# Sparse attention stage of a fused two-block kernel: the attention jobs begin inside the turning of the query heads, the compressed branch is cut into pieces between jobs, and a small product moves from VectorE to GpSimd

## The chip, the cores and the metric

One core of one Trainium2 chip runs the whole program. The metric is device time in microseconds (us), median of the runs shown. Engines: TensorE (PE) with its weight loads (PEld), VectorE (DVE), ScalarE (ACT), GpSimd (POOL), and SyncE (SP), which issues the weight DMAs.

## The reference, cut to what matters

The program computes two transformer-like blocks on 256 tokens of width 1024. The change touches one mixer of the second block, a sparse attention of 16 query heads (64 wide) over 4 key/value heads with three branches and a gate for each:

```
qg = u @ w_qg
q = _rmsnorm(qg[..., :N_HEADS * HEAD_DIM].reshape(...), q_norm)
gates = jax.nn.sigmoid(qg[..., N_HEADS * HEAD_DIM:].reshape(...))
o_cmp, p_slc = _compressed_branch(q, k_cmp, v_cmp, rel_bias)   # 15 blocks of keys
o_slc = _selected_branch(q, k_slc, v_slc, idx, rel_bias)       # here all 4 blocks of 64 are selected
o_win = _window_branch(q, k_win, v_win, rel_bias)              # window 512 > 256 tokens
o = gates[..., 0:1] * o_cmp + gates[..., 1:2] * o_slc + gates[..., 2:3] * o_win
return o.reshape(bsz, seq, D_MODEL) @ w_o
```

With 256 tokens the selected and the window branch are both plain causal attention, each with its own keys and values; the compressed branch attends to 15 compressed keys.

## The kernel before, in words

The tokens are two tiles (t = 0, 1) of 128. Matmuls with weights are done in three passes of split float32 (hi and lo parts); the attention is in float32. Weights come in units of 128x1024 elements through a ring of 6: SP loads a unit once its slot's `w_hi` and `w_lo` are made, ACT makes `w_hi` (`hi_parts`, L330), DVE makes `w_lo` (`lo_parts`, L338), PE uses it (`pe_chunk`, L386 to L388).

The order of the work of each engine is written out by hand; the engines wait for one another through semaphores (`done` and `when`). PSUM has 8 banks, taken in turn from three pools: A (banks 0 to 3), S (4, 5) and T (6, 7). A bank is taken again only after its last reader.

The stage (`pe_nsa`, `act_nsa`, `dve_nsa`):

1. PE projects queries and gates (chunks `qg.0`, `qg.1`, `qg.gates`, the last one 48 columns wide). DVE normalizes the queries.
2. `pe_heads` (L868): 16 transposes in four groups `nsa.q` 0 to 3, through the T banks; ACT copies each group out to `qT` (`heads_out`, L877), labels `nsa.qT0` to `nsa.qT3`. Meanwhile DVE makes `w_lo` of five units of the next weights (L2845).
3. Compressed scores: 16 matmuls with all 128 rows, in two T banks (L2738; each float32 matmul has two records). DVE adds the bias, takes the maximum and subtracts it (L2854 to L2860), ACT takes exp (L2803), DVE sums, inverts, multiplies with the gate and scales (`compressed_scaled`, L2871 to L2877).
4. 32 jobs (`nsa_jobs`), 16 for tile 0 with 128 keys and then 16 for tile 1 with 256 keys. A job is a pair of heads in one of the two branches (br). For each: PE scores (`pe_scores`, L523, 64 rows, both heads, one S bank each), DVE bias and maximum (`dve_max`, L557, L560), ACT exp (`act_exp`, L543), DVE reciprocal and its product with the gate (`dve_scale`, L576, L581), POOL scales the probabilities (`pool_attend`, L593), PE turns them (`pe_turn`, L532), ACT copies them out (`act_turned`, L601), PE multiplies with the values (`pv`, L2750, 64 columns wide) into the output banks. Both S banks are written by each job, so scores of job j+1 wait for L557 of job j.
5. `pe_attend` interleaves: scores of job j+3, then an optional piece from `between[j]`, then the turn of job j, then values of job j-1. In `between[0]` stand the compressed probabilities' transposes (L2761), in `between[1]` the 32 matmul records of the compressed output (L2771), which also start the output banks. `dve_attend` runs `between[j]`, `dve_scale(j)`, `dve_max(j+2)`; `act_attend` runs `act_exp(j+2)`, `between[j]`, `act_turned(j)`.
6. ACT and DVE split the output banks into `x_hi` and `x_lo` (L2814, L2883), and PE multiplies with `w_o` (chunks `wo_nsa.0` and `.1`).

Of the kernel before, what the change touches and what calls it, by code (L numbers as in the profile page):

```python
# [12 lines left out]
ALU = mybir.AluOpType  # L13
# [3 lines left out]
P = 128  # L17
# [103 lines left out]
def build(nc, book, d, out, bias_rows):  # L121
    ctx = ExitStack()
    done, when = book.done, book.when
    with ctx:
# [444 lines left out]
        def dve_scale(dve, tag, j, job):  # L569

            dve.wait_ge(*when(f"{tag}.exp{j}.1"))
            if job["late"] is not None:
                nc.vector.reciprocal(job["late"], soft[:, j % len(job["slots"]), 0, 1, :]).then_inc(*done("softmax_dve", f"{tag}.r{j}"))
                return
            r = soft[:, j % len(job["slots"]), 1, 2, :]
            nc.vector.reciprocal(r, soft[:, j % len(job["slots"]), 0, 1, :]).then_inc(*done("softmax_dve", f"{tag}.r{j}"))  # L576
            dve.wait_ge(*when(f"{tag}.r{j}"))
            if job["gate"] is not None:
                r2 = soft[:, j % len(job["slots"]), 1, 1, :]

                nc.vector.tensor_tensor(r2, r, job["gate"], ALU.mult).then_inc(*done("softmax_dve", f"{tag}.g{j}"))  # L581
                return
            for i in range(2):
                p = slot(j, job, 1)[:, i, 0:job["nk"]]
                nc.vector.tensor_scalar(p, p, r[:, i:i + 1], None, ALU.mult
                                        ).then_inc(*done("softmax_dve", f"{tag}.p{j}.{i}"))

        def pool_attend(pool, tag, jobs):

            for j, job in enumerate(jobs):  # L590
                pool.wait_ge(*when(f"{tag}.g{j}"))
                p = slot(j, job, 1)[:, :, 0:job["nk"]]
                nc.gpsimd.tensor_tensor(p, p, bc(soft[:, j % len(job["slots"]), 1, 1, :], 2, job["nk"]), ALU.mult  # L593
                                        ).then_inc(*done("softmax_pool", f"{tag}.p{j}.1"))
# [9 lines left out]
        def pe_attend(pe, tag, jobs, pv, between={}):  # L604
# [4 lines left out]
            for j in range(m):  # L609
# [250 lines left out]
        def pe_heads(pe, tag, src, n, width, ready):  # L860

            for a in range(n // 2):
                for x in ready(a) if callable(ready) else ready if a == 0 else ():
# [1841 lines left out]
        def nsa_jobs():  # L2705
            assert SEQ // 64 <= 8 and SEQ <= 512
            jobs = []
            for t in range(T):
                for a in range(NH // 2):
                    for br in range(2):  # L2710
# [5 lines left out]
                            late=None, bias=BT[:, 2 * a:2 * a + 2, SEQ - nk:SEQ], slots=slots_nsa, ready=[], a=a, t=t, br=br))  # L2716
# [8 lines left out]
        def pe_nsa(pe):  # L2725
# [3 lines left out]
            pe_heads(pe, "nsa.q", lambda t, i: q_nat2[:, t, i * P:(i + 1) * P], NH // 2, P,  # L2729
                     lambda a: [f"nsa.qn{a}"])  # L2730

            pe.wait_ge(*when("nsa.qT3"))
            pe.wait_ge(*when("cmp.kT1"))
            for t in range(T):
                b = take(pe, "T", f"cmp.scores{t}")
                for a in range(NH // 2):
                    o = psum[:, b, 32 * a:32 * a + 32].rearrange("p (i c) -> p i c", i=2)
                    last = nc.tensor.matmul(o[:, :, 0:n_blocks(t)], qT[:, a, t * P:(t + 1) * P],  # L2738
                                            kcTz[:, :, NCMP * (a // 2):NCMP * (a // 2) + n_blocks(t)], start=True, stop=True)
                last.then_inc(*done("cmp_pe", f"cmp.s{t}"))  # L2740
            o_banks = [[take(pe, "A", f"nsa.o{t}{x}") for x in range(2)] for t in range(T)]
            jobs = nsa_jobs()

            def pv(pe, j):
# [3 lines left out]
                for i in range(2):  # L2748
                    for kb in range(nb):
# [3 lines left out]
                            start=False, stop=True, skip_group_check=True)  # L2753
                return last

            def compressed_turn():
                for t in range(T):
                    pe.wait_ge(*when(f"cmp.p{t}"))
                    b = take(pe, "T", f"cmp.ptb{t}")
                    for x in range(2):  # L2760
                        last = nc.tensor.transpose(psum[:, b, x * P:(x + 1) * P],  # L2761
                                                   xc[:, t, 8 * x:8 * x + 8, :].rearrange("p h c -> p (h c)"), ident[:])
                    last.then_inc(*done("cmp_pe", f"cmp.pt{t}"))

            def compressed_out():
                pe.wait_ge(*when("cmp.pT1"))
                pe.wait_ge(*when("cmp.vc1"))

                for t in range(T):
                    for a in range(NH // 2):  # L2770
                        nc.tensor.matmul(psum[:, o_banks[t][a // 4], (a % 4) * P:(a % 4 + 1) * P],  # L2771
                                         vcz[:, 2 * a:2 * a + 2, :].rearrange("p i d -> p (i d)"), pcT[:, t, a // 4, :],
                                         start=(a % 4 == 0), stop=True, skip_group_check=True)

            pe_attend(pe, "nsa.sm", jobs, pv, between={0: compressed_turn, 1: compressed_out})
# [4 lines left out]
        def act_nsa(act):  # L2780
# [19 lines left out]
            for t in range(T):  # L2800
# [3 lines left out]
            def compressed_turned():  # L2804
                for t in range(T):
                    act.wait_ge(*when(f"cmp.pt{t}"))
                    nc.scalar.activation(pcT[:, t], bank(f"cmp.ptb{t}")[:, 0:2 * P].rearrange("p (a k) -> p a k", a=2), ACT.Copy
                                         ).then_inc(*done("cmp_act", f"cmp.pT{t}", frees=(f"cmp.ptb{t}",)))

            act_attend(act, "nsa.sm", nsa_jobs(), between={0: compressed_turned})  # L2810
# [10 lines left out]
        def dve_nsa(dve):  # L2821
# [23 lines left out]
            lo_parts(dve, chunk_end("qg.gates") + RING - 1)  # L2845
            dve.wait_ge(loads["bias_in"], 16 * P // SHIFTED)
            dve.wait_ge(*when("nsa.xc0"))
            dve.wait_ge(*when("nsa.late"))
            for t in range(T):
# [11 lines left out]
            def compressed_scaled():  # L2861
                for t in range(T):
                    x = xc[:, t, :, 0:n_blocks(t)]
                    m, r = cm[:, 2 * t], cm[:, 2 * t + 1]
    
                    def step(ins, label):
                        ins.then_inc(*done("cmp_dve", label))
                        dve.wait_ge(*when(label))
    
                    dve.wait_ge(*when(f"cmp.e{t}"))  # L2870
                    step(nc.vector.tensor_reduce(m, x, AX.X, ALU.add), f"cmp.sum{t}")  # L2871
                    step(nc.vector.reciprocal(r, m), f"cmp.r{t}")
                    dve.wait_ge(*when("nsa.gate1"))
                    step(nc.vector.tensor_tensor(m, r, gate[:, t, :, 0], ALU.mult), f"cmp.g{t}")
                    if t == 0:
                        step(nc.vector.tensor_scalar(m, m, late, None, ALU.mult), "cmp.late")
                    step(nc.vector.tensor_tensor(x, x, bc(m, 2, n_blocks(t)), ALU.mult), f"cmp.p{t}")  # L2877

            dve_attend(dve, "nsa.sm", nsa_jobs(), between={0: compressed_scaled})
# [152 lines left out]
```

## Time and profile before

| what | value |
|---|---|
| median of 3 runs | 1487.38 us (1486.51 to 1488.74) |
| profiled execution | 1487.94 us, its span 1486.2 us |
| PE busy | 1409.9 us, 95% of the span |
| DVE, ACT, POOL busy | 851.4, 807.4, 325.4 us |
| mean granted TensorE clock | 0.963 |

The span is the time from the first to the last instruction of the profiled execution; the time around it is 1.7 us. The stage that is changed lies between 1190 and 1272 us of the span. A TensorE clock of 1.00 is 2.4 GHz, of 0.50 is 1.2 GHz.

### The profile page before, as it was taken

How to read it: one execution, taken by the hardware profiler on the slowest of the kernel's cores; microseconds unless marked ns; L12 is line 12 of the kernel's file. 1: busy time of each engine (PE TensorE's matmuls, PEld its weight loads, DVE VectorE, ACT ScalarE, POOL GpSimd, SP SyncE). 2: the span in 40 equal slices, each digit the busy share in tenths (PEclk: the TensorE clock that was granted, in tenths of full speed). 3: DMA queues.
4: the chain of work that ended last, by engine and by line, in shares of the span. 5: the costliest groups of instructions: out<-in, count | busy, mean ns of one | idle time of the engine just before them, and what ended most of it. 6: DMA issues, size and time to landing. Idle time of an engine off the chain costs nothing.

```text
span 1486.2 us, 21916 instructions
## 1 busy us (share of the span) xinstructions
PE 1409.9 (95%) x7306; PEld 1164.9 (78%) x7306; DVE 851.4 (57%) x1240; ACT 807.4 (54%) x1322; POOL 325.4 (22%) x368
## 2 busy tenths in 40 slices
PE   8998989999879999959899999999999989999998
PEld 6887878887758887848778888888888875788887
DVE  5537665446566655657665555555555569455554
ACT  7776566674665555322664444765444548464442
POOL 2011000011159979927310000010000005000000
PEclk9998999999989999966899999999999969999999
DMA  9532535522455654210685565478656420356661
GB/s 333 170 95 72 212 114 179 154 92 76 138 142 188 190 164 136 99 29 15 207 263 185 185 191 188 153 158 219 192 185 193 137 72 2 114 184 186 195 185 56
DMA packets 170926, 224.73 MB, mean 151 GB/s; under 512 B 15881, under 2 KB 113393, under 8 KB 170849
## 3 DMA queue, kind: packets, MB, share of 16 engines
q1 hardware_dynamic: 168016, 217.27, 46.0%
q0 software_dynamic: 2160, 6.02, 2.6%
q8 instruction: 47, 0.77, 0.2%
q10 hardware_dynamic: 672, 0.42, 0.1%
q14 instruction: 31, 0.25, 0.1%
HBM read 221.16 MB, written 1.44 MB: 150 GB/s over the span
## 4 chain that ended last, share of the span: by engine, by line
PE 84%; DVE 7%; ACT 4%; POOL 3%; issue 2%; DMA 0%; SPq 0%; ACTq 0%; DVEq 0%; POOLq 0%
PE psum L1609 14%; PE psum L1597 11%; PE psum L1599 11%; PE psum L1598 11%; PE psum L386 8%; PE psum L388 8%; PE psum L387 8%; PE psum L523 2%; PE psum L412 2%; DVE w_lo L338 1%; PE psum L1636 1%; POOL w_raw L2017 1%; PE psum L532 1%; PE psum L2750 1%; PE psum L2550 1%
## 5 line engine op out<-in xcount | busy, mean ns | idle before, releaser
L1796 DVE TENSOR_TENSOR w_lo<-w_raw,w_hi 128x1024 fp32r<-128x1024 f32 x216 | 283.8, 1315 | 288.1 <-ACT w_hi L1730 287.8
L1730 ACT ACTIVATE w_hi<-w_raw 128x1024 fp32r<-128x1024 f32 x216 | 228.8, 1060 | 309.3 <-PE psum L1599 217.4
L338 DVE TENSOR_TENSOR w_lo<-w_raw,w_hi 128x1024 fp32r<-128x1024 f32 (+4 forms) x191 | 225.6, 1208 | 121.5 <-ACT w_hi L330 120.2
L1597 PE MATMUL psum<-w_hi,x_hi 128*128 128x512 f32 x704 | 280.8, 399 | 1.5 <-DVE x_lo L438 0.7
L1599 PE MATMUL psum<-w_hi,x_lo 128*128 128x512 f32 x704 | 275.3, 391 | 0.0
L1598 PE MATMUL psum<-w_lo,x_hi 128*128 128x512 f32 x704 | 274.8, 390 | 0.0
L330 ACT ACTIVATE w_hi<-w_raw 128x1024 fp32r<-128x1024 f32 (+4 forms) x191 | 193.2, 1038 | 109.8 <-PE psum L388 63.1
L386 PE MATMUL psum<-w_hi,x_hi 128*128 128x512 f32 (+5 forms) x608 | 232.9, 383 | 3.3 <-DVE x_lo L2883 2.3
L388 PE MATMUL psum<-w_hi,x_lo 128*128 128x512 f32 (+5 forms) x608 | 228.3, 375 | 0.0
L387 PE MATMUL psum<-w_lo,x_hi 128*128 128x512 f32 (+5 forms) x608 | 227.9, 375 | 0.0
L1599 PEld LDWEIGHTS psum<-w_hi,x_lo 128*128 128x128 f32 x704 | 132.5, 188 | 28.6
L1597 PEld LDWEIGHTS psum<-w_hi,x_hi 128*128 128x128 f32 x704 | 132.6, 188 | 28.2 <-issue 1.3
L1598 PEld LDWEIGHTS psum<-w_lo,x_hi 128*128 128x128 f32 x704 | 132.8, 189 | 26.0
L386 PEld LDWEIGHTS psum<-w_hi,x_hi 128*128 128x128 f32 x608 | 115.7, 190 | 24.0 <-DVE x_lo L2883 2.6
L388 PEld LDWEIGHTS psum<-w_hi,x_lo 128*128 128x128 f32 x608 | 115.7, 190 | 20.3
L387 PEld LDWEIGHTS psum<-w_lo,x_hi 128*128 128x128 f32 x608 | 115.9, 191 | 18.3
L1609 PE MATMUL psum<-w_hi,f_hi 128*128 128x512 f32 x320 | 100.6, 396 | 3.1 <-DVE f_lo L1790 3.1
L1609 PE MATMUL psum<-w_lo,f_hi 128*128 128x512 f32 x320 | 99.1, 391 | 0.0
L1609 PE MATMUL psum<-w_hi,f_lo 128*128 128x512 f32 x320 | 99.1, 391 | 0.0
L593 POOL TENSOR_TENSOR arena<-arena,soft 128x256 f32<-128x256 f32 (+1 forms) x32 | 26.5, 827 | 246.7 <-DVE soft L581 246.7
L438 DVE SCALAR_TENSOR_TENSOR x_lo<-psum,gain,x_hi 128x256 fp32r<-128x256 f32 x104 | 44.4, 476 | 47.4 <-ACT x_hi L422 47.4
L1609 PEld LDWEIGHTS psum<-w_hi,f_hi 128*128 128x128 f32 x320 | 59.5, 190 | 15.3 <-DVE f_lo L1790 3.5
(404 smaller groups left out, 1823.3 us busy)
## 6 DMA issues: line engine op xcount, KB each, us to landing
w_raw<-in_ffn_w_in SPq DMA_DIRECT2D x352, 256.0 KB, 3.2
w_raw<-in_ffn_w_out SPq DMA_DIRECT2D x176, 256.0 KB, 2.8
w_raw<-in_w_in SPq DMA_DIRECT2D x88, 256.0 KB, 3.5
w_raw<-in_w_out SPq DMA_DIRECT2D x32, 256.0 KB, 3.7
w_raw<-in_w_kv SPq DMA_DIRECT2D x24, 256.0 KB, 2.9
w_raw<-in_mem_wk SPq DMA_DIRECT2D x16, 256.0 KB, 5.7
w_raw<-in_mem_wv SPq DMA_DIRECT2D x16, 256.0 KB, 4.8
w_raw<-in_mem_wq SPq DMA_DIRECT2D x16, 256.0 KB, 6.3
```

Of the source, the lines that this page charges most:

```text
L330: nc.scalar.activation(w_hi[:, s, 0:size(u)], w_raw[:, s, 0:size(u)], ACT.Copy).then_inc(hi_ready, 1)
L338: nc.vector.tensor_tensor(w_lo[:, s, 0:size(u)], w_raw[:, s, 0:size(u)], w_hi[:, s, 0:size(u)].bitcast(F32), ALU.subtract).then_inc(lo_rea ...
L386: nc.tensor.matmul(o, xh, whi, start=(k + i == x_first), stop=False)
L387: nc.tensor.matmul(o, xh, wlo, start=False, stop=False)
L388: last = nc.tensor.matmul(o, xl, whi, start=False, stop=(k + i == x_first + kts - 1))
L438: ins = nc.vector.scalar_tensor_tensor(lo, pb, g[:, k:k + 1], hi, ALU.mult, ALU.subtract)
L1597: nc.tensor.matmul(o, xh, whi, start=(kt == 0), stop=False)
L1598: nc.tensor.matmul(o, xh, wlo, start=False, stop=False)
L1599: last = nc.tensor.matmul(o, xl, whi, start=False, stop=(kt == KT - 1))
L1609: last = nc.tensor.matmul(psum[:, FF_ACC[2 * t + n], :], x, w[:, n * 512:(n + 1) * 512], start=(first and w is whi and x is xh), stop=Fals ...
L1730: nc.scalar.activation(w_hi[:, s, :], w_raw[:, s, :], ACT.Copy).then_inc(hi_ready, 1)
L1796: nc.vector.tensor_tensor(w_lo[:, s, :], w_raw[:, s, :], w_hi[:, s, :].bitcast(F32), ALU.subtract).then_inc(lo_ready, 1)
```

## The change

- `pe_heads` gets a `between` argument. Scores of job 0 are issued before group 2 of the query transposes, scores of job 1 before group 3, and `pe_attend` begins with job 2 (`begun=2`). Jobs of tile 0 and branch 0 wait for their `nsa.qT` group.
- The compressed scores go into two A banks (which later serve as the output banks of tile 1) in four pieces at jobs 2 to 5; the transposes of the compressed probabilities at jobs 11 and 13; the compressed output in four pieces at jobs 13 to 16. The first value matmul of tile 0 in each bank now starts the bank.
- ACT and DVE do their parts of the compressed branch at the jobs shown.
- DVE makes two units of `w_lo` instead of five before the attention; the other three follow after it.
- The product of reciprocal and gate is done by POOL, just before its scaling, instead of DVE.

```diff
@@ dve_scale
             nc.vector.reciprocal(r, soft[..., 0, 1, :]).then_inc(*done("softmax_dve", f"{tag}.r{j}"))
+            if job["gate"] is not None:
+                return
             dve.wait_ge(*when(f"{tag}.r{j}"))
-            if job["gate"] is not None:
-                r2 = soft[:, j % len(job["slots"]), 1, 1, :]
-                nc.vector.tensor_tensor(r2, r, job["gate"], ALU.mult).then_inc(*done("softmax_dve", f"{tag}.g{j}"))
-                return
@@ pool_attend
+                pool.wait_ge(*when(f"{tag}.r{j}"))
+                nc.gpsimd.tensor_tensor(g, r, job["gate"], ALU.mult).then_inc(*done("softmax_pool", f"{tag}.g{j}"))
                 pool.wait_ge(*when(f"{tag}.g{j}"))
@@ pe_attend
-            for j in range(m):
+            for j in range(begun, m):
                 pe_scores(pe, tag, j, jobs[j])
@@ nsa_jobs
-                            ... ready=[], a=a, t=t, br=br))
+                            ... ready=[f"nsa.qT{a // 2}"] if t == br == 0 else [], a=a, t=t, br=br))
@@ pe_nsa
-            pe_heads(pe, "nsa.q", ..., lambda a: [f"nsa.qn{a}"])
-            (all compressed scores here, in two T banks)
+            pe_heads(pe, "nsa.q", ..., lambda a: [f"nsa.qn{a}"],
+                     between={2: lambda: pe_scores(pe, "nsa.sm", 0, jobs[0]), 3: lambda: pe_scores(pe, "nsa.sm", 1, jobs[1])})
+            score_bank = [take(pe, "A", f"cmp.scores{t}") for t in range(T)]
+            o_banks = [[take(pe, "A", f"nsa.o0{x}") for x in range(2)], score_bank]
...
-                            start=False, stop=True, skip_group_check=True)
+                            start=(t == 0 and a % 4 == 0 and job["br"] == 0 and kb == 0), stop=True, skip_group_check=True)
...
-            pe_attend(pe, "nsa.sm", jobs, pv, between={0: compressed_turn, 1: compressed_out})
+            compressed = {2: lambda: compressed_scores(0, 0), 3: lambda: compressed_scores(0, 1),
+                          4: lambda: compressed_scores(1, 0), 5: lambda: compressed_scores(1, 1),
+                          11: lambda: compressed_turn(0), 13: lambda: [compressed_turn(1), compressed_out(0, 0)],
+                          14: lambda: compressed_out(0, 1), 15: lambda: compressed_out(1, 0), 16: lambda: compressed_out(1, 1)}
+            pe_attend(pe, "nsa.sm", jobs, pv, between=compressed, begun=2)
@@ act_nsa
-            act_attend(act, "nsa.sm", nsa_jobs(), between={0: compressed_turned})
+            act_attend(act, "nsa.sm", nsa_jobs(), between={6: lambda: compressed_exp(0), 8: lambda: compressed_exp(1),
+                                                           12: lambda: compressed_turned(0), 14: lambda: compressed_turned(1)})
@@ dve_nsa
-            lo_parts(dve, chunk_end("qg.gates") + RING - 1)
+            lo_parts(dve, chunk_end("qg.gates") + 2)
...
-            dve_attend(dve, "nsa.sm", nsa_jobs(), between={0: compressed_scaled})
+            dve.wait_ge(*when("nsa.gate1"))
+            dve_attend(dve, "nsa.sm", nsa_jobs(), between={5: lambda: compressed_max(0), 7: lambda: compressed_max(1),
+                                                           9: lambda: compressed_scaled(0), 11: lambda: compressed_scaled(1)})
```

`compressed_scores(t, half)` is 4 of the 8 compressed score matmuls of tile t, `compressed_out(t, x)` 4 of its 8 output matmuls, `compressed_turn(t)` its two transposes; the operations themselves are those of before.

## Rows read from the trace of the kernel before

**Rows 1.** The page: PE busy, and the granted clock in 40 slices.
```profile
PE 1409.9 (95%) x7306; PEld 1164.9 (78%) x7306; DVE 851.4 (57%) x1240; ACT 807.4 (54%) x1322; POOL 325.4 (22%) x368
...
PEclk9998999999989999966899999999999969999999
```

**Rows 2.** Stretches: length, busy us (instructions) of each engine, granted clock, DMA.
```profile
668.00:688.00 20.00, 19.78 (x127) 17.79 (x128) 15.08 (x22) 3.71 (x7) 15.08 (x14) 0.50 0.00 1
139.30:149.40 10.10, 10.05 (x36) 8.66 (x36) 6.96 (x17) 6.40 (x26) 4.60 (x3) 0.50 0.27 56
1193.96:1200.79 6.83, 6.81 (x33) 6.30 (x33) 6.36 (x13) 4.69 (x8) 0.00 (x0) 0.50 0.02 4
1204.20:1221.27 17.07, 12.07 (x57) 10.06 (x57) 9.55 (x33) 5.27 (x21) 2.46 (x4) 0.50 0.29 95
1221.27:1272.40 51.13, 47.72 (x411) 29.91 (x411) 40.69 (x115) 43.04 (x148) 24.00 (x28) 1.00 0.01 1
1272.47:1275.88 3.41, 3.41 (x10) 2.65 (x9) 0.47 (x1) 0.00 (x0) 0.00 (x0) 0.50 0.41 121
```

**Rows 3.** Timeline of PE: start, length, operation, idle time before.
```profile
1197.32 3.77 PE L868 MATMUL psum<-ident,arena 128*128 128x128 f32 x16
1201.86 4.93 PE L2738 MATMUL psum<-arena 128*128 128x14 f32 x32 [0.78 <-ACT arena L877]
...
1213.97 0.80 PE L523 MATMUL psum<-arena 64*128 64x128 f32 x4 [3.03 <-DVE arena L557]
...
1215.96 0.66 PE L532 MATMUL psum<-ident,arena 128*128 128x128 f32 x2
...
1217.28 5.73 PE L2771 MATMUL psum<-arena 128*128 128x128 f32 x32
1222.84 0.38 PE L532 MATMUL psum<-ident,arena 128*128 128x128 f32 x2
```

**Rows 4.** Compressed scores (L2738) at full clock: length, PE busy (records), clock.
```profile
1201.86:1204.20 2.34, 2.34 (x21) 1.00 0.93 283
```

**Rows 5.** Compressed output (L2771) at half clock, same columns.
```profile
1217.85:1221.27 3.42, 3.42 (x18) 0.50 0.00 0
```

**Rows 6.** The chain of waits, one tile-0 job, and the first turn of tile 1.
```profile
1224.01 0.37 PE psum L532 x2
1224.38 0.37 PE psum L2750 x4
1224.75 0.42 PE psum L523 x4
...
1241.77 0.59 PE psum L532 x4
```

**Rows 7.** Timeline of DVE.
```profile
1198.40 5.76 DVE L338 TENSOR_TENSOR w_lo<-w_raw,w_hi 128x1024 fp32r<-128x1024 f32 x5
...
1206.83 0.56 DVE L2854 SCALAR_TENSOR_TENSOR arena<-psum,arena 128x240 f32<-128x240 f32 x1 [1.80 <-PE psum L2738]
...
1208.18 0.42 DVE L557 SCALAR_TENSOR_TENSOR arena<-psum,arena 128x256 f32<-128x256 f32 x1
...
1211.75 0.40 DVE L2871 TENSOR_REDUCE arena<-arena 128x16 f32<-128x240 f32 x1
...
1213.13 0.17 DVE L576 RECIPROCAL soft<-soft 128x2 f32<-128x2 f32 x1
...
1226.21 0.16 DVE L581 TENSOR_TENSOR soft<-soft,arena 128x2 f32<-128x2 f32 x1
```

**Rows 8.** Timeline of ACT.
```profile
1201.83 1.28 ACT L2803 ACT_TABLE_LOAD   x1
...
1209.08 0.40 ACT L543 ACTIVATE arena<-arena,soft 128x128 f32<-128x128 f32 x1 [0.38 <-DVE soft L560]
```

**Rows 9.** POOL's groups by shape: busy us, mean ns, idle before.
```profile
L593 POOL TENSOR_TENSOR arena<-arena,soft 128x256 f32<-128x256 f32 x16 | 9.8, 614 | 235.3 <-DVE soft L581 235.3
L1935 POOL TENSOR_SCALAR arena<-arena 128x1 f32<-128x1 f32 x1 | 0.2, 187 | 0.1
```

More of the change, by code:

```diff
@@ L858, in pe_mem_kv, with pe_heads @@
             pe_heads(pe, f"memk{l}", lambda t, i: mk_nat[:, t, i * P:(i + 1) * P], MEM_H, P, [f"memk{l}.nat1"])
-        def pe_heads(pe, tag, src, n, width, ready):
+        def pe_heads(pe, tag, src, n, width, ready, between={}):
             for a in range(n // 2):
+                if a in between:
+                    between[a]()
                 for x in ready(a) if callable(ready) else ready if a == 0 else ():
@@ L2728, in pe_nsa @@
             pe_chunk(pe, "qg.gates")
[L2729 to L2741, printed above, removed]
             jobs = nsa_jobs()
+            pe_heads(pe, "nsa.q", lambda t, i: q_nat2[:, t, i * P:(i + 1) * P], NH // 2, P, lambda a: [f"nsa.qn{a}"],
+                     between={2: lambda: pe_scores(pe, "nsa.sm", 0, jobs[0]), 3: lambda: pe_scores(pe, "nsa.sm", 1, jobs[1])})
+            score_bank = [take(pe, "A", f"cmp.scores{t}") for t in range(T)]
+            o_banks = [[take(pe, "A", f"nsa.o0{x}") for x in range(2)], score_bank]
             def pv(pe, j):
@@ L2765, in compressed_out @@
[L2765 to L2773, printed above, removed]
@@ L2775, in pe_nsa, with compressed_scores @@
-            pe_attend(pe, "nsa.sm", jobs, pv, between={0: compressed_turn, 1: compressed_out})
+            def compressed_scores(t, half):
+                if t == half == 0:
+                    pe.wait_ge(*when("nsa.qT3"))
+                    pe.wait_ge(*when("cmp.kT1"))
+                for a in range(4 * half, 4 * half + 4):
+                    o = psum[:, score_bank[t], 32 * a:32 * a + 32].rearrange("p (i c) -> p i c", i=2)
+                    last = nc.tensor.matmul(o[:, :, 0:n_blocks(t)], qT[:, a, t * P:(t + 1) * P],
+                                            kcTz[:, :, NCMP * (a // 2):NCMP * (a // 2) + n_blocks(t)], start=True, stop=True)
+                if half:
+                    last.then_inc(*done("cmp_pe", f"cmp.s{t}"))
@@ new lines, in compressed_turn, with compressed_out @@
+            def compressed_turn(t):
+                pe.wait_ge(*when(f"cmp.p{t}"))
+                free_bank(pe, score_bank[t], f"cmp.ptb{t}")
+                for x in range(2):
+                    last = nc.tensor.transpose(psum[:, score_bank[t], x * P:(x + 1) * P],
+                                               xc[:, t, 8 * x:8 * x + 8, :].rearrange("p h c -> p (h c)"), ident[:])
+                last.then_inc(*done("cmp_pe", f"cmp.pt{t}"))
+            def compressed_out(t, x):
+                if x == 0:
+                    pe.wait_ge(*when(f"cmp.pT{t}"))
+                    pe.wait_ge(*when("cmp.vc1"))
+                if t:
+                    free_bank(pe, o_banks[t][x], f"nsa.o{t}{x}")
+                for a in range(4 * x, 4 * x + 4):
+                    nc.tensor.matmul(psum[:, o_banks[t][x], (a % 4) * P:(a % 4 + 1) * P],
+                                     vcz[:, 2 * a:2 * a + 2, :].rearrange("p i d -> p (i d)"), pcT[:, t, x, :],
+                                     start=(t == 1 and a % 4 == 0), stop=True, skip_group_check=True)
@@ L2799, in act_nsa, with compressed_exp @@
             heads_out(act, "act", "nsa.q", qT, NH // 2, P, "nsa.qT", scale=gcol["qk"][:, 0:1])
-            for t in range(T):
+            def compressed_exp(t):
                 act.wait_ge(*when(f"cmp.sub{t}"))
```

60 lines of the change are left out of this document (26 added, 34 removed).

## The prediction

> **What bounds the kernel now.** I read the page first: PE is busy 95% of the span, and the clock line falls to 6 in the slice that holds the changed stage [rows 1]. Then the stretches with their clock, then the timelines of the stage. From 1193.96 to 1272.40 two regimes are seen. From 1204.20 to 1221.27 TensorE has 1.2 GHz and works 12.07 of 17.07 us; from 1221.27 on it has 2.4 GHz and works 47.72 of 51.13 us [rows 2]. In the first regime little is done: the compressed scores (4.93 us), four job scores with waits up to 3.03 us for L557, and the compressed output (5.73 us) [rows 3]. In the second the chain of waits runs on PE alone: turn 0.37, values 0.37, scores 0.42, so 1.16 us for a tile-0 job [rows 6]. So until the turn of job 1 at 1222.84 latency and the low clock bound the stage, and after it PE's own work does. From the turn of job 1 to that of job 16 (1241.77) it is 18.9 us, 15 x 1.16 = 17.4 plus 1.5 where the tile changes [rows 3, 6].
>
> **The start.** Eight query transposes at 3.77/16 = 0.24 us, the scores of job 0 at 0.80, four transposes: PE is at about 1201.0. DVE, with two conversions of 5.76/5 = 1.15 us instead of five, is free at 1200.7, does L557 (0.42), and lets the scores of job 1 go at 1201.2 [rows 3, 7]. At full clock these take 0.42 [rows 6], the last four transposes (half of 0.94) 0.5, and PE has finished them and the scores of job 2 by 1202.7. ACT's last copy-out then ends about 1203.0, where it ended at 1201.8; the table load (1.28) moves with it, so the first exp is at 1204.3 instead of 1209.08 [rows 8]. Two exps (0.8), reciprocal (0.17), L557 (0.42): the scores of job 3 at 1205.8, and the turn of job 0 at 1206.6, where it was 1215.96 [rows 3, 7, 8]. The turn of job 1 follows at 1208.0, where it was 1222.84 [rows 3]. That is 14.8 us earlier. It is not the gain: all compressed pieces are still to come.
>
> **What is put back between the jobs, at full clock.** Compressed scores: 32 records at 2.34/21 = 0.11 us, 3.6 us [rows 4]. Compressed transposes: four, as two tile-0 turns, 0.7 us [rows 6]. Compressed output: 32 records, 0.19 us each at half clock [rows 5], so 0.10 to 0.11 at full, 3.5 us. DVE: both S banks are refilled by each job, so what DVE does between two L557 delays PE's next scores unless PE has something else. The first maximum piece lies beside PE's compressed scores, free. The second costs 1208.18 - 1206.83 = 1.35 us and each scaling piece 1213.13 - 1211.75 = 1.38 [rows 7]; DVE's own work for a job is about 0.9 of the 1.16, so about 1.1 us of each shows on PE, 3.3 us. Where all is hidden it is 0, where nothing is 4.1. The output pieces at jobs 13 to 16 cover the 1.5 us of the tile change. Sum: 3.6 + 0.7 + 3.5 + 3.3 - 1.5 = 9.6, so the turn of job 16 comes 14.8 - 9.6 = 5.2 us earlier. The 16 jobs of tile 1 are unchanged.
>
> **The same at half clock.** Here a tile-0 job costs scores 0.80, turn 0.66 [rows 3], and values, which no row shows at half clock: between 0.37 (the row at full clock) and twice that; I take 0.70, since the other two nearly double. That is 2.16 us. A job with a compressed score piece costs 8 x 0.21 = 1.7 more, 3.9 us (0.21 is twice rows 4). So from the turn of job 1 at 1208.0 four such steps lead to the turn of job 5 at 1223.5, and every further tile-0 job loses 1.0 us against before. The DVE pieces (about 0.9 + 1.38 = 2.3 in a job) nearly vanish beside 2.16. If the clock rises at the turn of job 6 (about 1225), the rest at full clock brings the turn of job 16 to 1243.9, 2.2 us later than before. If it rises only when the full-width output products come at jobs 13 and 14, it is at 1251, 9.5 us later. One at job 9 gives 4.3, one at jobs 10 to 11 gives 6.6.
>
> **Which of the two.** The clock before the change falls twice here: at 1193.96 after matmuls 48 columns wide that fully occupied PE, and at 1204.20 after a wait of 0.78 us and matmuls of 14 columns [rows 2, 3]. It rises twice: at 1200.79 after full-width transposes back to back, and at 1221.27 after the 128x128 output products had run back to back since 1217.28 [rows 2, 3, 5]. After the change PE has about 1.7 us of transposes and scores of 64 rows between 1200.8 and 1202.7, then it waits until 1205.8 for the first exp. I expect the clock to fall at 1204.20 as before. And what follows is narrow: scores of 64 rows, values 64 columns wide, compressed scores of 14 and 30 columns. Being busy isn't enough: from 668 to 688 PE was busy 19.78 of 20 us and stayed at 0.50, and in the attention at 139.30 to 149.40 10.05 of 10.10 us at 0.50 [rows 2]. What raised the clock before was the block of output products, and the change cuts that block up and puts it last. So the likeliest is half clock through jobs 2 to 5 and on for some jobs more, with the rise between job 6 and job 14: the end 2.2 to 9.5 us later. I take the middle, 6 us later.
>
> The Trainium skill, TensorE: Matmul & The Clock Gate, "What's actually happening", says that sustained activity releases the throttle. By it the low clock would end soon after the jobs run densely; that is a rival below. Rows 2 at 668 and 139.30 speak against it. The same page, "PE-mode transpose", says that transposes don't count as busy for the gate. The trace disagrees: the rise at 1200.79 came after transposes alone.
>
> **The smaller parts.** POOL's product on two elements isn't in the trace. Its nearest row is 0.187 us for one column; the upper bound is a whole scaling, 0.614 [rows 9]. I take 0.19. It replaces 0.16 on DVE [rows 7], so the probabilities are ready about 0.1 us later (up to 0.5), and POOL has 0.61 + 0.19 plus a short wait of 1.16, so it hides; at the end of the last job 0.1 shows. DVE's relief of 0.2 us a job gains nothing on a chain that runs on PE, at most 0.3 where DVE paces the tile change. The three conversions moved behind the attention, 3.5 us of DVE [rows 7], and the six DMAs of their ring slots, lie beside the `w_o` products: ten matmuls took 3.41 us at half clock [rows 2], so two ready units of 12 matmuls last at least 4 us even at full clock, and the third is converted 1.2 us after DVE is free. Cost 0; if the cover were gone, 3.5. The later loads are wanted six units on. The half-clock stretch at 1272.47 to 1275.88 [rows 2] may come or not with the shifted end: plus or minus 1.7. `between[0]` and `between[1]` are empty now, their waits are gone, with what stood behind them (turns of jobs 0 and 1), counted above.
>
> The Trainium skill, SBUF — State Buffer, "SBUF: two separate sides", says that a DVE instruction with two SBUF inputs and a GpSimd instruction block each other on a shared port pair. Six compressed DVE instructions of this kind now lie beside POOL's 0.61 us. As an estimate by that rule they could add up to 6 x 0.6 = 3.7 us, and the end would be 9 to 10 us later instead of 6. No row of before shows the two together.
>
> **Rivals.**
>
> - *The clock stays up.* If the startup's work at 1200.8 to 1202.7 and from 1205.8 on suffices, or the low clock ends at once, PE gets the sum at full clock: 5.2 us earlier (3.8 if it is low until the turn of job 2), about 1482.5. For it: the dense tile-0 jobs from 1224 on held 1.00 [rows 2]. Against it: the wait of 3 us, and the compressed score pieces. 17%. The skill's rule of sustained activity leads to the same times by another road; I give that road 8% more.
> - *A draw.* The clock rises just as the score pieces end, at job 3 to 6. Later jobs gain back what the start lost: between 2.2 earlier and 2.3 later, about 1487.5. 15%.
> - *The clock doesn't come back at all in the attention.* Then each tile-1 job would cost nearly double its 1.8 us, 16 x 1.6 = 26 us, about 1522. The output products at jobs 13 to 16 speak against it. 3%.
> - *The DVE to POOL hand-over becomes the bound*: 0.5 us per job where POOL's small product costs 0.6; 32 jobs x 0.1 to 0.3 exposed, 3 to 9 us on top of whichever clock. POOL's 0.187 row speaks against it. 4%, and it would end slower.
>
> **How the numbers follow.** The likeliest case (about 53%): the profiled execution's 1487.94 plus 6 is 1493.9; it stood 0.56 above the median of the runs, so 1493.4 for a median. Its own range is 1489.5 to 1498. The range with the other cases goes from 1482.5 (clock up) to 1499 (rise at job 14, or the port rule's and the POOL bound's additions); about 1 in 5 lies outside. 0.2% is 3.0 us, about what a measurement of this kernel can tell from no change. Faster by more: 25%, nearly all of it the clock rival. Within: the draw and the early edge of the likeliest case, 18%. Slower: 57%.
>
> **What would show it.** Right: the clock rows of the changed kernel have 0.50 from 1204 to beyond 1225, the turn of job 0 near 1206.6, tile-0 jobs 2.2 us apart and 3.9 with score pieces, tile-1 jobs again 1.82. Wrong: 1.00 from 1207 or 1211 on with jobs 2 to 5 about 2.05 us apart; POOL's small product above 0.3 us; PE waiting for POOL in front of L532; waits for `w_lo` after 1270.

## The result and the profile after

| | before | after |
|---|---|---|
| median of 7 runs (lowest to highest) | 1486.51 us (1483.48 to 1490.37) | 1495.26 us (1489.70 to 1497.98) |
| profiled execution, span | 1487.94 us, 1486.2 us | 1495.26 us, 1493.6 us |
| mean granted TensorE clock | 0.963 | 0.955 |
| PE busy | 1409.9 us | 1420.3 us |
| stage: first matmul 48 columns wide to first `w_o` matmul | 81.4 us | 88.8 us |

The changed kernel is slower by half a per cent: ratio 1.0048, 95% interval 1.0033 to 1.0064. 1493.4 us was forecast. In the two profiled executions the stage accounts for the whole difference of the spans: 1190.44 to 1271.85 us before, 1190.64 to 1279.46 after, 7.4 us more.

The page of the changed kernel, to be read beside [rows 1]: PE is busy for 10.4 us more with the same 7306 matmuls, so the matmuls themselves got longer. The clock line has 5 and 8 in the two slices of the stage where it had 6 and 9.

```profile
PE 1420.3 (95%) x7306; PEld 1170.7 (78%) x7306; DVE 844.7 (57%) x1208; ACT 807.3 (54%) x1322; POOL 331.9 (22%) x400
...
PEclk9998999999989999967899999999999958999999
```

The stretches of the changed kernel answer to [rows 2] (length, busy us and instructions of PE, PEld, DVE, ACT, POOL, then the granted clock). Before, two stretches at 0.50 were 6.83 and 17.07 us long. Now there is one of 47.79 us, and PE works 44.92 us of it:

```profile
1193.76:1241.55 47.79, 44.92 (x218) 31.38 (x218) 26.44 (x76) 25.64 (x90) 12.01 (x30) 0.50 0.07 23
1241.55:1279.10 37.55, 34.69 (x305) 22.77 (x303) 24.86 (x52) 29.50 (x89) 20.53 (x34) 1.00 0.01 1
1279.10:1282.50 3.40, 3.04 (x7) 2.48 (x8) 3.40 (x4) 0.00 (x0) 0.00 (x0) 0.50 0.14 34
```

The chain of waits of the changed kernel shows the steps one by one. First the beginning, then a job with a score piece, a job without one, the first output products (L2775), beside which the clock rises, and a job of tile 1:

```profile
1204.22 1.28 ACT L543
1205.50 0.01 issue
1205.52 0.89 ACT arena L543 x4
...
1207.06 0.80 PE psum L523 x4
1207.86 0.62 PE psum L532 x2
...
1213.52 0.63 PE psum L2743 x4
1214.15 0.73 PE psum L523 x4
1214.88 1.81 PE psum L2755 x8
1216.70 0.51 PE psum L532 x2
...
1232.46 0.63 PE psum L2743 x4
1233.08 0.73 PE psum L523 x4
1233.81 0.62 PE psum L532 x2
...
1241.20 1.12 PE psum L2775 x8
1242.32 0.22 PE psum L532 x2
...
1251.27 0.59 PE psum L2743 x8
1251.87 0.63 PE psum L523 x4
1252.50 0.59 PE psum L532 x4
```

The turn of job 0 is at 1207.8, 8.2 us ahead of the 1215.96 before [rows 3]. The turn of job 16 is at 1249.1, 7.4 us behind the 1241.70 before. Between the two a job without a piece takes 1.97 us (values 0.63, scores 0.73, turn 0.62), not 1.16 [rows 6], and one with a score piece 3.68. From job 16 on both kernels take 1.82 us a job.

### The profile page after: what moved, and what is told of

It is laid out like the page before. It is cut to its first block, busy times and chain, and to the rows that moved or that the text cites. A ratio compares the mean times of both kernels' runs of the same rounds, so it can differ in the third digit from the quotient of the medians.

```text
span 1493.6 us, 21915 instructions
## 1 busy us (share of the span) xinstructions
PE 1420.3 (95%) x7306; PEld 1170.7 (78%) x7306; DVE 844.7 (57%) x1208; ACT 807.3 (54%) x1322; POOL 331.9 (22%) x400
## 4 chain that ended last, share of the span: by engine, by line
PE 84%; DVE 6%; ACT 4%; POOL 3%; issue 2%; DMA 1%; SPq 0%; ACTq 0%; DVEq 0%; POOLq 0%
PE psum L1611 14%; PE psum L1599 11%; PE psum L1601 11%; PE psum L1600 11%; PE psum L386 8%; PE psum L388 8%; PE psum L387 8%; PE psum L523 2%; PE psum L412 2%; DVE w_lo L338 1%; PE psum L532 1%; PE psum L1638 1%; POOL w_raw L2019 1%; PE psum L2743 1%; PE psum L2552 1%
## 5 line engine op out<-in xcount | busy, mean ns | idle before, releaser
L1798 DVE TENSOR_TENSOR w_lo<-w_raw,w_hi 128x1024 fp32r<-128x1024 f32 x216 | 280.7, 1301 | 290.7 <-ACT w_hi L1732 290.5
L1611 PEld LDWEIGHTS psum<-w_hi,f_lo 128*128 128x128 f32 x320 | 60.6, 189 | 12.9
```

The source lines that it names most:

```text
L1611: last = nc.tensor.matmul(psum[:, FF_ACC[2 * t + n], :], x, w[:, n * 512:(n + 1) * 512], start=(first and w is whi and x is xh), stop=Fals ...
L1798: nc.vector.tensor_tensor(w_lo[:, s, :], w_raw[:, s, :], w_hi[:, s, :].bitcast(F32), ALU.subtract).then_inc(lo_ready, 1)
```

## The experiments

One figure is used for all: the length of the stage in the profiled execution, from the first matmul 48 columns wide to the first `w_o` matmul. It leaves out what an execution gained or lost before the stage (its beginning lay between 1184.4 and 1191.8 us of the span, in code that is the same for all), which the whole times hold. It is still the figure of a single execution, and one kernel's executions differ in where the clock falls and rises: the third kernel, whose PE does the work of before in the same order, has 82.9 us beside 81.4, and the fifth and sixth, which are the same up to the last value product, have 77.9 and 91.8. So the medians and their intervals have to be read beside it. "Useless product" is a 128x128x512 matmul on `x_hi` in a bank whose content is overwritten or not yet in use; nobody reads it. Each ratio is to the kernel before on the same chip. In a line of PE, `64*128 64x128` gives rows and columns of the operand that is loaded into the array, then rows and columns of the one that is streamed through it; the rows are the rows of the array that the matmul uses.

| kernel | stage us | at 0.50 in the stage, up to the `w_o` matmuls | median us | ratio, 95% |
|---|---|---|---|---|
| before | 81.4 | 6.8 + 17.1 | 1486.5 to 1488.1 | |
| after | 88.8 | 47.8 | 1495.26 | 1.0033 to 1.0064 |
| 1 wait filled | 85.8 | 10.2 + 27.3 | 1490.74 | 1.001 to 1.0044 |
| 2 wait and all jobs filled | 80.3 | 13.7 | 1483.10 | 0.9965 to 0.9996 |
| 3 gate product alone | 82.9 | 27.3 | 1487.02 | 0.9982 to 1.0015 |
| 4 beginning alone | 83.1 | 27.3 | 1486.21 | 0.9979 to 1.001 |
| 5 wait and jobs 2 to 5 filled | 77.9 | 10.2 | 1479.75 | 0.9944 to 0.9975 |
| 6 as 5, and the end filled | 91.8 | 6.8 + 37.6 | 1481.88 | 0.9944 to 0.9976 |
| 7 before, its waits filled | 78.7 | 6.8 + 10.2 | 1484.99 | 0.9967 to 0.9994 |
| 8 outputs cut, scores whole | 88.5 | 47.8 | 1493.83 | 1.0022 to 1.0051 |
| 9 jobs 2 to 5 filled alone | 94.1 | 54.6 | 1496.39 | 1.0054 to 1.0087 |
| 10 as 5, DVE's waits filled | 79.3 | 10.2 | 1482.66 | 0.9965 to 0.9994 |
| 11 as 5, over 64 rows | 95.1 | 54.6 | 1501.09 | 1.005 to 1.0104 |
| 12 one block at job 6 | 87.8 | 34.1 | 1490.72 | 1.0011 to 1.0043 |

**1 and 2: is it the clock?** The first fills the wait for the first exponentials of the changed kernel, the second adds products to the jobs of tile 0 too.

```diff
-            pe_attend(pe, "nsa.sm", jobs, pv, between=compressed, begun=2)
+            pe_scores(pe, "nsa.sm", 2, jobs[2])
+            fill(pe, score_bank[0], 7)       # 7 useless products
+            pe_attend(pe, "nsa.sm", jobs, pv, between=compressed, begun=3)
@@ pe_turn, the second kernel only, ahead of its wait
+        FILLS = lambda j: 2 if 2 <= j < 6 else 1 if j < 16 else 0
+            for _ in range(FILLS(j) if job["gate"] is not None else 0):
+                (useless product into the bank of the turn)
```

> The changed kernel with the scores of job 2 issued ahead of the loop and, behind them, seven 128x128 matmuls of 512 columns on query inputs that are lying there, into a PSUM bank whose content is overwritten later. They fill the 2.85 us in which PE waits for the first exp; nothing uses them. Theory (the low clock is the cost, and it stays low because the work is narrow): the clock rises near 1207.4 instead of 1241.5, jobs 2 to 5 are about 2.05 us apart instead of 3.7. If it then holds, 5 us under the kernel before (about 1482); if the compressed score pieces bring it down again, 1486 to 1492, still under the changed kernel's 1495. Rival A (cutting and moving the pieces costs by itself, through waits and DVE's pieces between the jobs, and the clock is a by-product): useless matmuls change nothing or add up to 1 us, 1495 to 1496.

> As the one before, and each turn of jobs 0 to 15 is preceded by one more such useless matmul (two at jobs 2 to 5) into the turn's own bank, 20 matmuls more. Theory (clock): 0.21 us each at full clock is 4.3 us of added PE work, part of it in waits; the clock is up from about 1207 to the end of the attention, and the turn of job 16 comes at about 1239 to 1241 instead of 1249; the total is 1484 to 1488. Rival A (order and waits): 27 useless matmuls at 0.21 to 0.43 us each are added, 1500 to 1503.

With more work in the wait the stage is 3.0 us shorter than in the changed kernel; the ratios to the kernel before are 1.0027 and 1.0048, but their intervals overlap. With more work in the jobs too the kernel is faster than before (1483.10, 0.9965 to 0.9996), an interval that just leaves out no change. The stretches and the timeline of PE in the first kernel show what each does. Seven products fill the wait, and the clock rises at 1202.10. It stays up over two pieces of compressed scores and is down again from 1208.99 until the output products:

```profile
1191.93:1202.10 10.17, 8.88 (x37) 6.63 (x37) 6.79 (x13) 6.70 (x12) 0.00 (x0) 0.50 0.32 103
1202.10:1208.99 6.89, 6.61 (x52) 4.64 (x50) 4.58 (x15) 5.32 (x25) 4.02 (x10) 1.00 0.01 2
1208.99:1236.30 27.31, 27.31 (x136) 17.61 (x136) 14.11 (x46) 13.59 (x57) 8.85 (x22) 0.50 0.00 1
```

```profile
1200.20 2.77 PE L2786 MATMUL psum<-x_hi 128*128 128x512 f32 x7
1203.13 0.49 PE L523 MATMUL psum<-arena 64*128 64x128 f32 x4 [0.15 <-DVE arena L557]
...
1205.76 1.06 PE L2755 MATMUL psum<-arena 128*128 128x14 f32 x8
...
1207.82 1.06 PE L2755 MATMUL psum<-arena 128*128 128x14 f32 x8
...
1210.47 1.91 PE L2755 MATMUL psum<-arena 128*128 128x30 f32 x8
```

In its low stretch PE is busy for 27.31 of 27.31 us, so it wasn't a wait that kept the clock down; in the 6.89 us before the fall PE was busy for 6.61. The same piece of eight scores takes 1.06 us on one side of the fall and 1.91 on the other.

**3 and 4: the other parts of the change, each alone on the kernel before.**

```diff
@@ 3: dve_scale / pool_attend
-                nc.vector.tensor_tensor(r2, r, job["gate"], ALU.mult)
+                nc.gpsimd.tensor_tensor(g, r, job["gate"], ALU.mult)
@@ 4: pe_nsa (compressed scores, turn and output whole, in their old places)
+            pe_heads(..., between={2: lambda: pe_scores(pe, "nsa.sm", 0, jobs[0]), 3: lambda: pe_scores(pe, "nsa.sm", 1, jobs[1])})
@@ 4: dve_nsa
-            lo_parts(dve, chunk_end("qg.gates") + RING - 1)
+            lo_parts(dve, chunk_end("qg.gates") + 2)
```

> The kernel before with one part of the change alone: the product of reciprocal and gate on POOL. Theory: it costs and gives nothing, because the chain of these jobs runs on PE: within 1 us of the kernel before. Rival B (the hand-over from DVE to POOL costs 0.1 to 0.3 us a job on the path, 32 jobs): 3 to 9 us slower, and a share of the 8.8 us that the change costs.

> The kernel before with another part alone: the scores of jobs 0 and 1 inside the query transposes, two conversions before the attention instead of five; the compressed scores, transposes and output products stay whole blocks where they were. Theory (the block of output products is what brings the clock back, near 1220): the clock rises about as before or one to two stretches earlier, the time is 1 to 5 us under the kernel before. Rival C (the scores inside the transposes spoil the rise at 1200.8, and that alone costs): the rise at 1200.8 is missing as in the changed kernel, and the time is 1 to 4 us over the kernel before. Rival A: faster by what the early beginning saves, and the clock as before.

Neither moved the time by more than can be told from noise: 1487.02 and 1486.21 beside 1487.17. I had given the beginning alone a gain of 1 to 5 us; that failed. The rise at 1200.8 is missing in it, as rival C had it, but it is missing in the third kernel too, where the sixteen transposes stand back to back as before:

```profile
1194.56 3.93 PE L868 MATMUL psum<-ident,arena 128*128 128x128 f32 x16 [0.56 <-DVE arena L2843]
```

```profile
1193.22:1220.53 27.31, 21.16 (x97) 18.12 (x97) 17.70 (x41) 11.52 (x30) 3.19 (x8) 0.50 0.31 97
```

So that rise comes in some executions and not in others, and the score groups among the transposes needn't be what stopped it. The timeline of PE in the fourth kernel shows why nothing was gained: the scores in advance run, but the scores of job 3 wait for DVE, which has the compressed work in front of L557, and the turn of job 0 is at 1215.90, where it was at 1215.96.

```profile
1201.89 7.03 PE L2745 MATMUL psum<-arena 128*128 128x14 f32 x32 [0.78 <-ACT arena L883]
1208.85 0.80 PE L523 MATMUL psum<-arena 64*128 64x128 f32 x4
1213.92 0.80 PE L523 MATMUL psum<-arena 64*128 64x128 f32 x4 [4.27 <-DVE arena L557]
1214.65 1.11 PE L2767 MATMUL psum<-ident,arena 128*128 128x128 f32 x4
1215.90 0.66 PE L532 MATMUL psum<-ident,arena 128*128 128x128 f32 x2
```

So the early beginning is worth nothing that can be measured while the compressed branch stays whole in its old place, and what costs the clock is what was done to that branch. Cutting it and moving it behind the narrow jobs weren't tried apart; the eighth kernel tells only that the scores needn't be cut for it.

**5: how little filling is enough.** As the first, with two products at each of jobs 2 to 5 (15 in all), none in later jobs.

> The changed kernel with the seven useless matmuls in the wait for the first exp, and two more at each of jobs 2 to 5, where the compressed scores are; none at jobs 6 to 15. Theory (clock; the score pieces are what brings it down again, as at 1209 in the run with the filled gap alone): it stays up through the attention, and without the other twelve the time is 1 to 2.5 us under that of the run that had them all (1483.1), 1480.5 to 1482. Rival D (the DVE pieces at jobs 7, 9 and 11, which make PE wait about 1 us each, bring the clock down too): it falls near job 7 or later and the time is 1486 to 1491.

Median 1479.75 us, 0.25 to 0.56% under the kernel before: this version beats both. The low stretch ends at 1201.20 and none follows until the end of the stage and beyond. That is one execution: of the twelve, seven took 1477.71 to 1479.79 us at a mean clock of 0.973 to 0.976, and five took 1483.93 to 1487.60 at 0.965 to 0.968. With the clock up, DVE's pieces show on PE as two waits, 0.76 and 0.53 us:

```profile
1190.99:1201.20 10.21, 9.11 (x38) 6.95 (x38) 6.99 (x14) 6.74 (x11) 0.00 (x0) 0.50 0.31 103
1201.20:1268.00 66.80, 61.53 (x501) 41.65 (x501) 47.26 (x115) 48.05 (x170) 32.65 (x64) 1.00 0.02 6
```

```profile
1219.22 0.49 PE L524 MATMUL psum<-arena 64*128 64x128 f32 x4 [0.76 <-DVE arena L560]
...
1222.39 0.49 PE L524 MATMUL psum<-arena 64*128 64x128 f32 x4 [0.53 <-DVE arena L560]
```

**6: the low stretch of the `w_o` matmuls.** Five more useless products behind the last value product.

```diff
+            for _ in range(5):
+                nc.tensor.matmul(psum[:, tail_bank, 0:SEQ], ident[:], BT[:, 0, :], start=True, stop=True)
```

> As the one before, and five more useless float32 matmuls of 256 columns behind the last value product, where PE waits 2.3 us for the split of the attention's output. Theory: the low stretch of 3.4 us that follows this wait (1272.5 before, 1279.1 in the changed kernel) doesn't come, and 1.7 us are saved: 1479 to 1481. Rival A: nothing saved, or up to 0.5 us lost because the last matmul is still running when the output is ready.

Inconclusive for the end, with a median above the 1479 to 1481 forecast: the interval is that of the fifth kernel, which in its profile had no low stretch there either. Its eight runs lie between 1478.37 and 1496.88, and the profile caught the longest. That one shows what can still go wrong: here the clock had risen at 1200.9, ahead of the filling, so the seven products took 1.88 us instead of 2.66 and left a wait of 1.05, and from 1207.7 to 1245.3 the clock was down, with the eight products of jobs 2 to 5 in that stretch. The other seven executions took 1478.37 to 1483.69.

```profile
1203.20 1.88 PE L2789 MATMUL psum<-x_hi 128*128 128x512 f32 x7
1206.13 0.49 PE L524 MATMUL psum<-arena 64*128 64x128 f32 x4 [1.05 <-DVE arena L560]
```

```profile
1207.72:1245.27 37.55, 37.55 (x174) 25.22 (x174) 16.81 (x54) 15.60 (x67) 11.21 (x28) 0.50 0.01 1
```

**7: the same cure for the kernel before.** Two, one and seven products behind the scores of jobs 0, 1 and 2.

> The kernel before with ten useless 512-column matmuls in the waits of its first job scores (two behind the scores of job 0, one behind job 1, seven behind job 2), nothing else. Theory (clock): it rises near 1211 to 1214 instead of 1221.3, and the block of output products takes 3.6 us instead of 5.7: 1.5 to 3.5 us under the kernel before, about 1484.5. Rival A: no gain, 1487 or up to 1 us more.

The clock rises at 1214.5 instead of 1221.3, the compressed output takes 3.84 us instead of 5.73 [rows 3], and the stage is 2.7 us shorter. The wait was there before the change too; the kernel before only paid less for it.

**8: which cutting did it.** The changed kernel, with the compressed scores whole ahead of job 2, and only the output in pieces.

```diff
+            for t in range(T):
+                for half in range(2):
+                    compressed_scores(t, half)
-            compressed = {2: lambda: compressed_scores(0, 0), ... 5: lambda: compressed_scores(1, 1),
+            compressed = {
```

> The changed kernel with the compressed scores whole again, as one block ahead of the job loop; the output products stay cut up at jobs 13 to 16. Theory (the whole block of output products ahead of job 1 is what brought the clock back before; dense tile-0 jobs alone don't): the clock stays at 0.50 until the output products, near 1240, and the time is 1492 to 1496, though no score piece stands between the jobs. Rival E (only the score pieces hold the clock down): it rises a few us after the jobs run densely, near 1218 to 1222, and the time is 1485 to 1488.

With no score piece between them the jobs of tile 0 ran 1.97 us apart, PE without a gap, for 25 us, and the clock stayed at 0.50 until 1242.50, behind the first output piece at 1239.93. So the pieces of scores aren't needed to keep it low; the attention's own matmuls over 64 rows or onto 64 columns don't raise it. Nor did all 32 records of compressed scores in one block, 7.01 us without a gap over all 128 rows but only 14 to 30 columns wide:

```profile
1204.47 7.01 PE L2755 MATMUL psum<-arena 128*128 128x14 f32 x32 [1.00 <-ACT arena L879]
```

```profile
1213.60:1239.00 25.40, 25.40 (x129) 14.29 (x128) 15.97 (x54) 16.88 (x71) 10.92 (x27) 0.50 0.00 1
```

**9 and 10: filling elsewhere.** The ninth has the eight products of jobs 2 to 5 and none in the wait. The tenth has three at jobs 2 to 5 and two at 7, 9 and 11, besides the seven.

> The changed kernel with two useless 128x128x512 products in each of jobs 2 to 5 and none in the wait for the first exponentials (eight in all). Clock theory: the beginning stays at 0.50, as in the changed kernel, and eight full-width products at half clock (about 0.43 us each there) bring the clock up during or just behind jobs 2 to 5, some 20 us earlier than the output products did; the jobs of tile 0 behind them then stand 1.44 us apart, not 1.97: ten to eleven jobs x 0.53 = about 5.5 us less, less about 1 to 2 us for products that do not fit beside a wait: 1489 to 1492 us. Rival (it is the beginning that decides, and what stands in the jobs is too little): half clock until the output products, and the eight products are paid in full, 3.4 us: 1497 to 1499 us.

> The kernel with the wait filled and two products at jobs 2 to 5, now with three there and two at each of jobs 7, 9 and 11, where TensorE waited 0.5 to 0.8 us for VectorE's pieces. Clock theory: ten more products of 0.21 us, of which six lie in waits; the clock that already stayed at 1.00 stays there, in more of the executions: 1479.5 to 1481 us. Rival (the useless products are now longer than the waits and TensorE is the bound): 2 us more than with fifteen, 1482 us or more.

The ninth went by its rival: 54.6 us at 0.50, longer than without filling, and 1496.39 us, just under the rival's 1497 to 1499. Two products in each job were enough to keep the clock up in the fifth but didn't bring it up here, nor in the profiled execution of the sixth. The expectation that the clock would rise during jobs 2 to 5 was wrong. The tenth brought no steadier clock and is 1.3 us longer in the stage than the fifth; its median is 2.9 us longer, on another chip: also by its rival.

**11: busy, or wide?** The fifth kernel, its fifteen products over 64 rows of the array instead of 128; same number, columns and length.

```diff
-nc.tensor.matmul(psum[:, b, :], x_hi[:, 0, 0:P], x_hi[:, 0:2, :]...)
+nc.tensor.matmul(psum[:, b, :], x_hi[0:64, 0, 0:P], x_hi[0:64, 0:2, :]...)
```

> The kernel with fifteen useless products (seven in the wait for the first exponentials, two at each of jobs 2 to 5), but each over 64 rows of the array instead of 128, same columns and so the same length. Theory of the width (what raises and holds the clock is full-width work, as the output products were): the filling at 64 rows does not raise the clock at 1201, it stays at 0.50 through jobs 2 to 5 and until the output products, and the useless products are paid on top: 1496 to 1501 us. Rival (it is the gap alone that matters: TensorE kept busy is enough, whatever the rows): the clock rises near 1201 as with 128 rows, 1479 to 1481 us.

```profile
1194.50:1248.90 54.40, 53.72 (x236) 35.92 (x238) 25.96 (x75) 26.66 (x94) 12.81 (x32) 0.50 0.07 20
```

The clock stayed at 0.50 with PE busy for 53.72 of 54.40 us, and the kernel is 0.5 to 1.0% slower than before, where the fifth is 0.25 to 0.56% faster. All five runs (1494.99 to 1501.40) are longer than all twelve of the fifth kernel (1477.71 to 1487.60). The one difference is the number of rows. Filling the wait with work is not what helps; filling it with these products over all rows is. All rows alone aren't enough either: the matmuls over 128 rows and 48 columns, back to back from 1190.44 on, are where the clock fell at 1193.96 before [rows 2], and the compressed scores above didn't raise it.

**12: one block, at another place.** Twelve products at job 6, none elsewhere.

> The changed kernel with twelve useless 128x128x512 products in one block at job 6, none elsewhere. Theory (full-width work in one block raises the clock wherever it stands): half clock up to the block, rise during or just behind it, near 1229 instead of 1241.5; the block costs 4 to 5 us, about six or seven jobs gain 0.8 us each: 1493 to 1496 us, and the clock rows show the rise at job 6 to 7. Rival (the rise with the output products had another reason, such as the copies beside them or the place in the kernel): no rise before the output products, and the block paid in full at half clock, 5.1 us: 1499 to 1501 us.

The block begins at 1227.16 and the clock is up at 1228.9; the twelve products take 3.83 us, and the next jobs are 1.1 to 1.2 us apart. The stage is 1.1 us shorter than in the changed kernel, although 3.8 us of useless work stand in it. The median, 1490.72, is under the 1493 to 1496 forecast; the profiled execution is the slowest of the ten. So a block of full-row matmuls brings the clock up in the middle of the jobs too, and a rise isn't tied to the place of the output products. That the output products did the same in the changed kernel is inferred. The clock rose about 0.5 us behind the start of the first piece there, and 2.0 to 3.5 us behind it in kernels 1, 6, 8, 9 and 11; the first scores 256 columns wide and the compressed transposes stand just ahead of that piece in all of them, and no run parts the three.

```profile
1226.43 0.80 PE L524 MATMUL psum<-arena 64*128 64x128 f32 x4
1227.16 3.83 PE L530 MATMUL psum<-x_hi 128*128 128x512 f32 x12
1230.82 0.38 PE L535 MATMUL psum<-ident,arena 128*128 128x128 f32 x2
1231.13 0.44 PE L2746 MATMUL psum<-arena 128*64 128x128 f32 x4
1231.50 0.49 PE L524 MATMUL psum<-arena 64*128 64x128 f32 x4
```

## Why the prediction was right

The mechanism was the predicted one: at 0.50 the narrow jobs take nearly double, and they don't bring the clock back by themselves. Experiments 2, 5, 8, 11 and 12 show it. 6 us more than before were forecast; the profiled executions differ by 7.4, the medians by 8.75. Step by step:

- **The start.** Forecast: turn of job 0 at 1206.6, that of job 1 at 1208.0. Measured: 1207.8 and 1209.2. The order of causes held (table load, exps, reciprocal, L557). What was off is the clock: I had it rise at 1200.8 as before, and it didn't, and the 16 transposes took 2.0 + 1.1 + 1.1 us. Why it didn't is open: in the third kernel it didn't either, without scores between the transposes, and in the sixth it rose at 1200.9 with them. I had forecast two low stretches with a full-clock piece between; there is one from 1193.76 on. This part of the prediction was wrong, and the turns of jobs 0 and 1 were 1.2 us late, 0.56 of it because the gates ended later in this execution (1197.88 beside the 1197.32 of [rows 3]).
- **The terms at half clock.** A job 2.16 forecast, 1.97 measured; with a score piece 3.9 and 3.68. The mis-sized terms are values (0.70 taken, 0.63 in the chain) and scores and turn, for which I took lengths of records (0.80, 0.66) where the chain has 0.73 and 0.62, since neighbours overlap. About 0.2 us too much per job, 2.4 us over twelve.
- **The rise.** Forecast between job 6 and 14; the middle, 6 us, lies between the prices of jobs 9 and 10. It came beside the first output products, at job 13, the late edge. The errors nearly cancel: 9.5 us for a rise at 13 and 14, less 2.4 for the shorter jobs, plus 1.2 for the start, is 8.3 beside the 7.4 measured; a rise with the first of these pieces rather than the second accounts for about one job's 0.8. The middle of the range had no cause of its own, and that it came so near was luck: in experiment 12 a full-row block raised the clock, and in experiment 8 nothing raised it ahead of the output products, so the place to forecast was where such a block stood. The runs' spread (1489.70 to 1497.98, with mean clocks from 0.962 down to 0.951) says that other executions were at 0.50 for a shorter or longer time; where, only the profiled one shows.
- **DVE's pieces.** Forecast to nearly vanish beside jobs of 2.16 us, and to show at full clock. The changed kernel has no wait on PE there. At full clock the fifth kernel shows 0.76 + 0.53 = 1.3 us, where I had 3.3: that term was too large by 2.0.
- **POOL's product.** 0.19 forecast, 0.196 measured. It costs nothing that can be told from noise (experiment 3, 0.9982 to 1.0015). The row of the changed kernel:

```profile
L590 POOL TENSOR_TENSOR soft<-soft,arena 128x2 f32<-128x2 f32 x32 | 6.3, 196 | 245.3 <-DVE soft L576 245.3
```

- **The conversions moved behind the attention.** No wait for `w_lo`. The first `w_o` matmul waits 2.54 us for L2897 (2.33 before), and the low stretch there is 3.40 us beside 3.41 [rows 2]:

```profile
1279.46 0.76 PE L386 MATMUL psum<-w_hi,x_hi 128*128 128x512 f32 x1 [2.54 <-DVE x_lo L2897]
```

- **The shared port.** The forecast gave the rule of the Trainium skill, SBUF — State Buffer, "SBUF: two separate sides", up to 3.7 us. It wasn't put to the test. None of the six compressed DVE instructions with two inputs overlaps an instruction of POOL in the changed kernel's profile; L2889, for one, runs from 1229.80 to 1230.08, and POOL, which waits for DVE's reciprocals, begins at 1230.23. So the prediction's premise, that the two lie beside each other, is what failed there. POOL's scalings of 128x256 average 613 ns, beside 614 [rows 9].
- **Sustained activity.** That low clock ends soon under dense work was the rival of the Trainium skill, TensorE: Matmul & The Clock Gate, "What's actually happening". The 25.40 us of full occupation in experiment 8 and the 53.72 in experiment 11 speak against it where activity means a busy engine. The prediction also held the rise at 1200.79 against what the Trainium skill, TensorE: Matmul & The Clock Gate, "PE-mode transpose", says, that transposes don't count as busy for the gate. That reading was too strong: matmuls of 48 columns fill the first half of that low stretch, and the same transposes in the third kernel, 3.93 us of them, raised nothing. This case decides neither way.
- **What the rival "the clock stays up" was worth.** It gave 1482.5 us, 5.2 less than before. The fifth kernel comes nearest to that case, with 10.2 us at 0.50 at the start and fifteen useless products in it: 1479.75, ratio 0.9959, and 3.5 us less in the stage. The chain of 14.8 us won and 9.6 put back was right in direction. Not all of this is the change's own: filling brought the kernel before 0.2% on the same chip (experiment 7, 0.998), so about 0.2% is left to the new order, little more than the noise, and the low clock turned that into a loss of 0.5%.

## What to carry to other kernels

- Before you cut a block of full-row matmuls into pieces or move it behind narrow ones, look at the granted clock in the stretch: the block may be what brings the clock up for everything behind it. Count the narrow work behind it at the length it has at 0.50.
- If a stretch of narrow matmuls runs at 0.50, put full-row matmuls nobody reads into a wait just ahead of it, one block to raise the clock and a few per job to hold it, and compare it with the same matmuls over 64 rows. Judge it by many executions: one profile can catch the clock on either side, as the fifth and sixth kernels did with the same filling.

## What was not expected of the hardware

- Fifteen matmuls over 128 rows and fifteen over 64 rows take the same time (a pair of them at 0.50 1.20 us in the ninth kernel, 1.22 in the eleventh), yet the medians are 1479.75 and 1501.09 us, and the stage took 77.9 us with the one and 95.1 with the other.
- What keeps the clock up doesn't bring it up: with two full-row products per job 1.00 lasted from 1201.20 on in the fifth kernel, where without them it fell at 1208.99 in the first; in the ninth the same two left it at 0.50.
- The same order of matmuls doesn't fix the clock. A low stretch ended behind sixteen transposes at 1200.79 before [rows 2] and in the seventh kernel, but not in the third; with two score groups among them it did not end in the changed kernel but did in the sixth. What decides it no run here shows.
